# Encoder layer on one core: first operands of the down projection, the output projection's weights and a third table moved to earlier places

## The chip, the core and the metric

The kernel runs on one core of one Trainium2 chip. The metric is the device time in microseconds (us) of one execution; each kernel's time is the median of several. TensorE is written PE, VectorE DVE, ScalarE ACT, GpSimd POOL and SyncE SP, as in the rows. SP and POOL issue the transfers (DMA) between HBM and SBUF, each on a queue of its own.

## What is computed

A transformer-like encoder layer over 2560 tokens (512 of one request, 2048 of another) of width 1024, all in float32:

```python
def encoder_layer(x, w_in, w_fourier, sink_logits, w_out, ln_mix_g, ln_mix_b,
                  w_ff1, w_ff2, ln_ffn_g, ln_ffn_b):
    proj = x @ w_in
    ...
    heads = jnp.concatenate([fourier_mix(u, w_fourier),
                             windowed_attention(q, k, v, sink_logits)], axis=-1)
    x = layer_norm(DEEPNORM_ALPHA * x + heads @ w_out, ln_mix_g, ln_mix_b)
    h = jnp.square(jax.nn.relu(x @ w_ff1))
    x = layer_norm(DEEPNORM_ALPHA * x + h @ w_ff2, ln_ffn_g, ln_ffn_b)
    return x
```

`fourier_mix` is the real part of a 2-D DFT over positions and 128 channels, then a 128x128 map for each of four groups; `windowed_attention` has 8 query heads of 64 over 2 key and value heads, blocks of 128 tokens and a window of 128 to each side. The width of the hidden layer is 4096.

## The kernel before

It runs six stages one after the other, each with its own instruction streams, tiles and semaphores: `embed_project` (names a_), `fourier` (b_), `attend` (c_), `mix_out` (d_), `mlp_up` (u_) and `mlp_down` (e_). All orders are written out by hand, and semaphores alone say who waits. A stage ends when every engine has come to its end; SP comes to its end only when its last stores have landed. Then the stage's semaphores are cleared, all engines meet at a barrier, and the next stage begins. Few transfers cross such a border: those that a `load_...` function, handed over by `build`, issues into a tile that outlives a stage.

Each product of float32 matrices is made of three matmuls (`split_mm`, lines 63 to 65): both operands are split into a rounded part (hi, a cast on ACT) and a rest (lo, a subtraction on DVE). So an operand that lands in a raw tile needs one ACT and one DVE instruction before PE can use it.

**fourier.** Each of five units folds its 128 channels (`fold`: four DVE operations of half the length, two small ones, four more, `fold_low` splits the result), multiplies by a channel matrix on PE (`channels`, results z, four for each unit, each split by `z_high` and `z_low`), and then by tables of cosines and sines (`positions`). The first unit needs four table tiles of 128x2050, one after the other; each is loaded by POOL, rounded by `table_high` and split by `table_low`. The raw tables have two slots, so the third waits until `table_low` of the first is done.

**attend.** SP loads the bias (1.5 MB), then stores the results of 20 blocks. POOL loads the queries two blocks ahead.

**mix_out.** SP loads the output projection's eight weight tiles (0.5 MB each), POOL the heads' tile of 128 tokens and the tokens' x, two ahead. `product` takes 48 matmuls for 128 tokens, `norm` normalises, `transpose` and `mix_quarters` make the operands of the next stage. ACT and DVE first split the heads of block 0, then the eight weights, then the heads of block 1.

**mlp_up and mlp_down** are one level of Strassen's scheme (Winograd's form): seven products of sums of quarters. `mlp_up` goes through three groups of tokens, 16 pairs of hidden columns in each; `h_sums` on DVE makes four sums of each pair's results, and SP stores them. The sums of pair n are made and stored during pair n+1, those of the very last pair after it, ahead of the border. `mlp_down` is 336 steps, each with one 128x512 (or 384) piece of h and one 128x512 piece of weights in one of R = 8 raw slots; `load(n)` issues the two transfers, `high` and `low` split, and PE makes 12 matmuls of it (9 in later groups).

The border between these two, on the side of `mlp_up`'s SP:

```python
            store_sums(LAST, NP * len(UP_GROUPS) - 1, NP - 1)
            sp.wait_ge(h_sum_st, 16 * (NP * len(UP_GROUPS) + 1))
            for c in h_st:
                sp.wait_ge(h_st[c], 16 * (NP * len(UP_GROUPS) + 1))
```

## Time and profile before

| what | us |
|---|---|
| median of 3 runs (2564.68 to 2567.26) | 2567.06 |
| the profiled execution, its own time | 2564.25 |
| its span, first to last instruction | 2562.6 |
| PE busy in the span | 2402.4 |
| DVE busy | 1597.0 |
| ACT busy | 1094.0 |
| POOL busy | 179.4 |

The span is divided among the stages as follows, by the first instruction of each: fourier from 342 us, attend from 462.07 (SP's issue of the bias), mix_out from 690, mlp_up from 966, mlp_down from 1780. PE's matmuls are pipelined, so its busy time counts overlaps; what matters is where it stands idle and what ended the idle time, which is printed in brackets behind an instruction. "PEclk" is the granted clock of PE: 1.00 is 2.4 GHz and 0.50 is 1.2 GHz.

### The profile page before, as it was taken

What the parts mean: (1) busy time and instruction counts of PE and PEld (TensorE: products, weight loads), DVE (VectorE), ACT (ScalarE), POOL (GpSimd) and SP (SyncE); (2) the same over time, 40 slices, a digit from 0 to 9 for tenths busy, and PEclk for the clock granted to TensorE, in tenths of its full rate; (3) what the DMA queues carried; (4) which work ended last, traced back from release to release, by engine and by line L of the source; (5) the groups of instructions that cost most, each with busy time, mean ns of one, the idle gap of its engine ahead of it and who ended that gap; (6) DMA issues with size and microseconds to landing.
All of it is one profiled execution on the core that took longest, in us unless ns stands there. A gap on an engine that the chain in (4) does not pass through costs nothing. (4 is left out here: it accounts for less than half of the span.)

```text
span 2562.6 us, 35326 instructions
## 1 busy us (share of the span) xinstructions
PE 2402.4 (94%) x12192; PEld 2097.6 (82%) x12192; DVE 1597.0 (62%) x2220; ACT 1094.0 (43%) x1740; POOL 179.4 (7%) x246
## 2 busy tenths in 40 slices
PE   4999969899799987999999999997999999999998
PEld 3888859799678865888889999997888888888886
DVE  7544156666456567666676666665546577669667
ACT  2111123688611115444455555554433334544442
POOL 1000000222112210000000000000000011001001
PEclk9999979899899998999999999998999999999999
DMA  7665335322345665555577676665876659877974
GB/s 280 252 264 225 125 139 174 91 75 69 115 146 209 245 252 206 211 214 198 228 270 248 231 286 235 247 241 190 273 260 192 195 168 321 263 226 228 320 227 138
DMA packets 217624, 543.04 MB, mean 212 GB/s; under 512 B 21360, under 2 KB 89840, under 8 KB 198064
## 3 DMA queue, kind: packets, MB, share of 16 engines
q1 hardware_dynamic: 200208, 476.92, 53.4%
q0 software_dynamic: 17312, 64.76, 8.1%
q8 instruction: 61, 1.00, 0.2%
q14 instruction: 43, 0.35, 0.0%
HBM read 361.24 MB, written 180.36 MB: 211 GB/s over the span
## 5 line engine op out<-in xcount | busy, mean ns | idle before, releaser
L1794 DVE TENSOR_TENSOR e_lo<-e_raw,e_hi 128x896 fp32r<-128x896 f32 (+1 forms) x336 | 378.6, 1135 | 259.9 <-ACT e_hi L1777 251.8
L1777 ACT CAST e_hi<-e_raw 128x896 fp32r<-128x896 f32 (+1 forms) x336 | 330.4, 983 | 427.2 <-PE e_bank L65 380.5
L63 PE MATMUL e_bank<-e_hi,e_lo 128*128 128x512 f32 x1120 | 436.7, 390 | 15.6 <-DVE e_lo L1794 15.6
L65 PE MATMUL e_bank<-e_hi 128*128 128x512 f32 x1120 | 436.4, 390 | 0.0
L64 PE MATMUL e_bank<-e_lo,e_hi 128*128 128x512 f32 x1120 | 436.4, 390 | 0.0
L63 PE MATMUL u_bank<-u_x_hi,u_wa_lo 128*128 128x384 f32 (+1 forms) x768 | 274.2, 357 | 29.2 <-DVE u_x_first L1414 20.1
L65 PE MATMUL u_bank<-u_x_hi,u_wa_hi 128*128 128x384 f32 (+1 forms) x768 | 272.9, 355 | 0.0
L63 PEld LDWEIGHTS e_bank<-e_hi,e_lo 128*128 128x128 f32 x1120 | 210.7, 188 | 59.7 <-DVE e_lo L1794 15.9
L65 PEld LDWEIGHTS e_bank<-e_hi 128*128 128x128 f32 x1120 | 210.6, 188 | 43.9
L64 PEld LDWEIGHTS e_bank<-e_lo,e_hi 128*128 128x128 f32 x1120 | 210.7, 188 | 43.7
L63 PE MATMUL u_bank<-u_x_hi,u_wb_lo 128*128 128x384 f32 (+1 forms) x576 | 203.9, 354 | 8.3 <-DVE u_x_rest L1414 8.3
L64 PE MATMUL u_bank<-u_x_first,u_wa_hi 128*128 128x384 f32 (+1 forms) x576 | 205.1, 356 | 0.0
L65 PE MATMUL u_bank<-u_x_hi,u_wb_hi 128*128 128x384 f32 (+1 forms) x576 | 203.5, 353 | 0.0
L64 PE MATMUL u_bank<-u_x_rest,u_wb_hi 128*128 128x384 f32 (+1 forms) x576 | 203.5, 353 | 0.0
L63 PEld LDWEIGHTS u_bank<-u_x_hi,u_wa_lo 128*128 128x128 f32 x768 | 146.0, 190 | 41.7 <-issue 21.1
L65 PE MATMUL a_bank<-a_xt_hi,a_w_hi 128*128 128x512 f32 x400 | 159.6, 399 | 0.0
L64 PE MATMUL a_bank<-a_xt_lo,a_w_hi 128*128 128x512 f32 x400 | 157.6, 394 | 0.0
L63 PE MATMUL a_bank<-a_xt_hi,a_w_lo 128*128 128x512 f32 x400 | 157.3, 393 | 0.0
L65 PEld LDWEIGHTS u_bank<-u_x_hi,u_wa_hi 128*128 128x128 f32 x768 | 145.7, 190 | 10.3
L63 PE MATMUL d_mix<-d_w_hi,d_h_lo 128*128 128x512 f32 x320 | 128.4, 401 | 20.5 <-DVE d_w_lo L1224 20.5
L300 ACT ACTIVATE a_stage<-a_bank 128x512 f32<-128x512 f32 x50 | 29.9, 598 | 248.7 <-PE a_bank L65 248.7
L862 DVE CUSTOM_DVE_ANT_0 c_prob<-c_sc,c_bias,c_neg_sink 128x384 f32<-128x384 f32 (+1 forms) x160 | 93.9, 590 | 63.5 <-PE c_sc L962 43.5
(192 smaller groups left out, 4338.1 us busy)
## 6 DMA issues: line engine op xcount, KB each, us to landing
u_w_raw<-w_ff SPq DMA_DIRECT2D x48, 1024.0 KB, 7.8
e_raw<-s_t SPq DMA_DIRECT2D x192, 256.0 KB, 3.7
e_raw<-s_h SPq DMA_DIRECT2D x224, 192.0 KB, 2.8
e_raw<-w_ff SPq DMA_DIRECT2D x144, 256.0 KB, 3.9
u_w_sum<-s_ws SPq DMA_DIRECT2D x32, 1024.0 KB, 4.8
e_raw<-s_h SPq DMA_DIRECT2D x112, 256.0 KB, 2.8
s_h<-u_h_sum SPq DMA_DIRECT2D x32, 768.0 KB, 7.0
s_h<-u_h SPq DMA_DIRECT2D x96, 192.0 KB, 2.3
```

Source lines behind the costliest of these rows:

```text
L63: tensor.matmul(out, w_lo, m_hi, start=first, stop=False, skip_group_check=again)
L64: tensor.matmul(out, w_hi, m_lo, start=False, stop=False, skip_group_check=again)
L65: return tensor.matmul(out, w_hi, m_hi, start=False, stop=last, skip_group_check=again)
L300: act.mul(stage[:, m % 5, :], bank[:, m % 8, :], QSCALE if is_q else 1.0).then_inc(stage_done, 1)
L862: dve.tensor_tensor_reduce(prob[:, h % 4, 0:w], sc[:, h % 2, 0:w], bias[:, h, kbs[0] * P:kbs[0] * P + w], 1.0, neg_sink[:, h:h + 1], ALU.a ...
L1777: act.copy(part(hi, n), part(raw, n)).then_inc(hi_done, 1)
L1794: dve.tensor_tensor(part(lo, n), part(raw, n), part(hi, n).bitcast(F32), ALU.subtract).then_inc(split, 1)
```

## The change

- **fourier**: the raw tables get a third slot, in the tile of the values (`vt_raw`), which holds the channel matrices until `ab_split` 2. POOL loads the third table then, and the others when the table two before has been split. On ACT and DVE the order of the first unit's work is changed: `table_high(1)` stands ahead of the first `z_high`, and the first half of `fold(1)` stands between the third and the fourth `z_low`, ahead of `table_low(3)`.
- **attend and mix_out**: the eight weight tiles are loaded by `attend`'s SP, right behind the bias, into a tile `d_place` that both stages share. `mix_out` splits four weights, the heads of block 0, the other four weights, the heads of block 1. It uses the identity matrix that is already in SBUF, and its scratch lies in `d_place` and in the keys' tile.
- **mlp_up and mlp_down**: the two raw weight slots of `mlp_up` lie in the values' and the queries' tile, and become the raw slots 0 to 3 of `mlp_down`. In the last two pairs SP loads the first four steps of `mlp_down` into them. The last pair's sums are made by `mlp_down`'s DVE, behind `low(8)`, and stored by its SP, behind `load(20)`. The waits for the last stores of `mlp_up` stand in `mlp_down`, ahead of the first load of the last group.

The core of the difference (the rest passes tiles and semaphores along):

```diff
-                if n >= 2:
-                    pool.wait_ge(t_split, n - 1)
-                pool.dma_start(table(n)[2], table_ds[job][i * P:(i + 1) * P, :]).then_inc(t_ld[n % 2], 16)
+                if n == 2:
+                    pool.wait_ge(ab_split, 2)
+                elif n > 2:
+                    pool.wait_ge(t_split, n - 2)
+                pool.dma_start(table(n)[2], table_ds[job][i * P:(i + 1) * P, :]).then_inc(t_ld[n % 3], 16)
...
             fold(0)
             fold_low(0)
             table_low(0)
-            z_low(0, 0)
+            z_low_of(0, 0)
             table_low(1)
-            z_low(0, 1)
+            z_low_of(0, 1)
             table_low(2)
+            z_low_of(0, 2)
+            fold_once(1)
+            z_low_of(0, 3)
             table_low(3)
-            fold(1)
+            fold_twice(1)
             fold_low(1)
...
             table_high(0)
             copy_bias(0)
+            table_high(1)
             z_high(0, 0)
-            table_high(1)
+            table_high(2)
             z_high(0, 1)
-            table_high(2)
             table_high(3)
             fold_high(1)
...
             sp.dma_start(bias[:], bias_d).then_inc(bias_in, 16)
+            load_w_out(sp)
...
-            split_heads(0)
             for k in range(KT):
+                if k == KT // 2:
+                    split_heads(0)
                 act.wait_ge(w_ld[k], 16)
                 act.copy(w_hi[:, k, :], w_raw[k]).then_inc(w_hi_done, 1)
             split_heads(1)
...
-            rest_of_heads(0)
             for k in range(KT):
+                if k == KT // 2:
+                    rest_of_heads(0)
                 dve.wait_ge(w_hi_done, k + 1)
...
                     if not (g == LAST and isinstance(p, int) and p == NP - 2):
                         load_w(n + 2, s, 0 if isinstance(p, int) and p == NP - 2 else p + 2)
+                    else:
+
+                        sp.wait_ge(h_st[11], 16 * (NP + 1))
+                        load_down(sp, s)
                 elif g < LAST:
                     load_w(n + 2, s, 1)
+                else:
+                    load_down(sp, s)
...
-            store_sums(LAST, NP * len(UP_GROUPS) - 1, NP - 1)
-            sp.wait_ge(h_sum_st, 16 * (NP * len(UP_GROUPS) + 1))
-            for c in h_st:
-                sp.wait_ge(h_st[c], 16 * (NP * len(UP_GROUPS) + 1))
...
-            h_sums(NP * len(UP_GROUPS) - 1, UP_GROUPS[LAST][1])
...
+def load_step(sp, step, slot, loaded, h_d, w2_d, t_d):
+
+    raw = {"B11": 0, "B21": 2, "B22": 3}
+    g, j, k = step
+    size, col = UP_GROUPS[g][1], first_pair(g) * P
+    _, a, b = DOWN_ORDER[j]
+    sp.dma_start(slot[:, 512 - size:512], h_d[H_ORDER.index(a), k * P:(k + 1) * P, col:col + size]).then_inc(loaded, 16)
+    src, at = (w2_d, raw[b]) if b in raw else (t_d, T_ORDER.index(b))
+    sp.dma_start(slot[:, 512:1024], src[k * P:(k + 1) * P, at * 512:at * 512 + 512]).then_inc(loaded, 16)
...
+            def store_last_sums():
+                size, col = UP_GROUPS[LAST][1], first_pair(LAST) * P
+                sp.wait_ge(h_summed, 1)
+                sp.dma_start(h_d[3:7, FF // 2 - P:FF // 2, col:col + size].rearrange("s p c -> p s c"),
+                             h_sum[:, :, 0:size]).then_inc(h_sum_st, 16)
...
-                load(n)
+                if (g, j, k) == (LAST, 0, 0):
+                    sp.wait_ge(h_sum_st, 16 * (NK * len(UP_GROUPS) + 1))
+                    for c in h_st:
+                        sp.wait_ge(h_st[c], 16 * (NK * len(UP_GROUPS) + 1))
+                if n >= len(raw_first):
+                    load(n)
+                if n == 20:
+                    store_last_sums()
...
+            def last_sums():
+
+                w = UP_GROUPS[LAST][1]
+                dve.wait_ge(h_sum_st, 16 * NK * len(UP_GROUPS))
+                dve.tensor_tensor(h_sum[:, 0, 0:w], h[:, 0, 1, 0:w], h[:, 1, 1, 0:w], ALU.add)
+                dve.tensor_tensor(h_sum[:, 2, 0:w], h[:, 0, 0, 0:w], h[:, 0, 1, 0:w], ALU.subtract)
+                dve.drain()
+                dve.tensor_tensor(h_sum[:, 1, 0:w], h_sum[:, 0, 0:w], h[:, 0, 0, 0:w], ALU.subtract)
+                dve.drain()
+                dve.tensor_tensor(h_sum[:, 3, 0:w], h[:, 1, 0, 0:w], h_sum[:, 1, 0:w], ALU.subtract
+                                  ).then_inc(h_summed, 1)
...
                 if n == R:
+                    last_sums()
                     dve.wait_ge(const_in, 32)
...
+                def load_w_out(sp):
+                    for k in range(KT):
+                        sp.dma_start(place[:, k * D:(k + 1) * D], d["w_out"][k * P:(k + 1) * P, :]
+                                     ).then_inc(w_out_ld[k], 16)
...
+            raw_first = [tile.rearrange("p b c -> p (b c)")[:, half * D:(half + 1) * D] for tile in w_raw for half in range(2)]
+
+            def load_down(sp, slot):
+                for n in (2 * slot, 2 * slot + 1):
+                    load_step(sp, (0, 0, n), raw_first[n], op_ld[n], s["h"], d["w_ff2"], s["t"])
```

DVE in fourier, from the second table's split (`b_t_lo` is a table's rest, `b_z_lo` a z's, `c_q_raw` and `b_ends` are written by the first half of a fold, `b_u_raw` by the second). Before:

```order
L490 TENSOR_TENSOR b_t_lo<-c_k_raw,b_t_hi 128x2050
L496 TENSOR_TENSOR b_z_lo<-b_bank,b_z_hi 128x512 x2
L490 TENSOR_TENSOR b_t_lo<-c_k_raw,b_t_hi 128x2050 x2
L458 TENSOR_TENSOR c_q_raw<-b_u_raw 128x512
L459 TENSOR_TENSOR c_q_raw<-b_u_raw 128x512
L461 TENSOR_TENSOR c_q_raw<-b_u_raw 128x512
L462 TENSOR_TENSOR c_q_raw<-b_u_raw 128x512
L463 TENSOR_TENSOR b_ends<-b_u_raw 128x1
L464 TENSOR_TENSOR b_ends<-b_u_raw 128x1
L467 TENSOR_TENSOR b_u_raw<-c_q_raw 128x512
```

and in the changed kernel:

```order
L500 TENSOR_TENSOR b_t_lo<-c_vt_raw,b_t_hi 128x2050
L509 TENSOR_TENSOR b_z_lo<-b_bank,b_z_hi 128x512
L465 TENSOR_TENSOR c_q_raw<-b_u_raw 128x512
L466 TENSOR_TENSOR c_q_raw<-b_u_raw 128x512
L468 TENSOR_TENSOR c_q_raw<-b_u_raw 128x512
L469 TENSOR_TENSOR c_q_raw<-b_u_raw 128x512
L470 TENSOR_TENSOR b_ends<-b_u_raw 128x1
L471 TENSOR_TENSOR b_ends<-b_u_raw 128x1
L509 TENSOR_TENSOR b_z_lo<-b_bank,b_z_hi 128x512
L500 TENSOR_TENSOR b_t_lo<-c_k_raw,b_t_hi 128x2050
L477 TENSOR_TENSOR b_u_raw<-c_q_raw 128x512
```

The z of the first unit are now split between the tables, and the first half of the second unit's fold stands ahead of the fourth table's split instead of behind it.

ACT at the start of mix_out (`d_h_hi` are the heads' rounded parts, `d_w_hi` the weights'). Before:

```order
L1147 CAST d_h_hi<-d_h_raw 128x1024
L1166 CAST d_w_hi<-d_mixed 128x1024 x7
L1166 CAST d_w_hi<-d_w_last 128x1024
L1147 CAST d_h_hi<-d_h_raw 128x1024 x3
L1155 COPY d_mixed<-d_turn 128x512
```

and now:

```order
L1178 CAST d_w_hi<-d_place 128x1024 x4
L1158 CAST d_h_hi<-d_h_raw 128x1024
L1178 CAST d_w_hi<-d_place 128x1024 x4
L1158 CAST d_h_hi<-d_h_raw 128x1024 x3
L1166 COPY d_place<-d_turn 128x512
```

Four of the weights stand ahead of the heads of block 0; on DVE the rests stand in the same order.

SP around the end of mlp_up (`s_h` is the hidden layer in HBM; in the changed kernel `c_k_raw` holds the results and sums, `c_vt_raw` and `c_q_raw` the raw slots). Before:

```order
L1349 DMA u_w_sum<-s_ws 128x2048
L1364 DMA s_h<-u_h_sum 128x4x384
L1358 DMA s_h<-u_h 128x384 x3
L1364 DMA s_h<-u_h_sum 128x4x384
L1358 DMA s_h<-u_h 128x384 x3
L1364 DMA s_h<-u_h_sum 128x4x384
L1280 UNCONDITIONAL_BRANCH
L1706 UNCONDITIONAL_BRANCH
L1715 DMA e_raw<-s_h 128x512
L1721 DMA e_raw<-w_ff 128x512
L1715 DMA e_raw<-s_h 128x512
L1721 DMA e_raw<-w_ff 128x512
```

and now:

```order
L1355 DMA u_w_sum<-s_ws 128x2048
L1662 DMA c_vt_raw<-s_h 128x512
L1664 DMA c_vt_raw<-w_ff 128x512
L1662 DMA c_vt_raw<-s_h 128x512
L1664 DMA c_vt_raw<-w_ff 128x512
L1370 DMA s_h<-c_k_raw 128x4x384
L1364 DMA s_h<-c_k_raw 128x384 x3
L1662 DMA c_q_raw<-s_h 128x512
L1664 DMA c_q_raw<-w_ff 128x512
L1662 DMA c_q_raw<-s_h 128x512
L1664 DMA c_q_raw<-w_ff 128x512
L1370 DMA s_h<-c_k_raw 128x4x384
```

Eight transfers of mlp_down stand ahead of the stores of the last two pairs, four in each, and the store of the last sums no longer stands ahead of the stage's end.

## Rows read from the trace of the kernel before

**Rows 1.** The page, busy time of PE, share of the span, instructions:

```profile
PE 2402.4 (94%) x12192; PEld 2097.6 (82%) x12192; DVE 1597.0 (62%) x2220; ACT 1094.0 (43%) x1740; POOL 179.4 (7%) x246
```

**Rows 2.** Timeline of PE: start, duration, instruction, [idle before <-releaser]:

```profile
374.29 0.39 PE L63 MATMUL b_bank<-b_t_hi,b_z_lo 128*128 128x258 f32 x1 [2.87 <-DVE b_t_lo L490]
380.86 0.37 PE L63 MATMUL b_bank<-b_ends_hi,b_ab_lo 128*128 128x2 f32 x1 [4.06 <-DVE b_f_lo L484]
...
702.88 0.77 PE L63 MATMUL d_mix<-d_w_hi,d_h_lo 128*128 128x512 f32 x1 [16.86 <-DVE d_w_lo L1224]
...
1787.21 0.80 PE L63 MATMUL e_bank<-e_hi,e_lo 128*128 128x512 f32 x1 [15.57 <-DVE e_lo L1794]
```

**Rows 3.** Timeline of DVE, first unit of fourier:

```profile
362.28 2.29 DVE L490 TENSOR_TENSOR b_t_lo<-c_k_raw,b_t_hi 128x2050 fp32r<-128x2050 f32 x1 [1.10 <-ACT b_t_hi L573]
...
374.16 0.69 DVE L458 TENSOR_TENSOR c_q_raw<-b_u_raw 128x512 f32<-128x512 f32 x1
...
376.86 0.69 DVE L467 TENSOR_TENSOR b_u_raw<-c_q_raw 128x512 f32<-128x512 f32 x1
...
379.59 2.35 DVE L484 TENSOR_TENSOR b_f_lo<-b_u_raw,b_f_hi 128x1024 fp32r<-128x1024 f32 x2
```

**Rows 4.** Timeline of ACT, first unit of fourier:

```profile
360.34 1.90 ACT L573 CAST b_t_hi<-c_k_raw 128x2050 fp32r<-128x2050 f32 x1
...
364.98 0.58 ACT L579 CAST b_z_hi<-b_bank 128x512 fp32r<-128x512 f32 x1 [1.97 <-PE b_bank L65]
...
370.01 1.90 ACT L573 CAST b_t_hi<-c_k_raw 128x2050 fp32r<-128x2050 f32 x1 [2.64 <-DMA c_k_raw<-table]
```

**Rows 5.** Timeline of ACT, start of mix_out:

```profile
699.30 1.04 ACT L1147 CAST d_h_hi<-d_h_raw 128x1024 fp32r<-128x1024 f32 x1 [12.65 <-DMA d_h_raw<-s_heads]
700.25 5.04 ACT L1166 CAST d_w_hi<-d_mixed 128x1024 fp32r<-128x1024 f32 x5
```

**Rows 6.** Timeline of DVE, start of mix_out:

```profile
701.52 5.76 DVE L1224 TENSOR_TENSOR d_w_lo<-d_mixed,d_w_hi 128x1024 fp32r<-128x1024 f32 x5
...
723.11 1.29 DVE L1189 SCALAR_TENSOR_TENSOR d_y<-d_xn,d_mix 128x512 f32<-128x512 f32 x2 [7.93 <-PE d_mix L65]
...
734.00 1.28 DVE L1189 SCALAR_TENSOR_TENSOR d_y<-d_xn,d_mix 128x512 f32<-128x512 f32 x2 [3.65 <-PE d_mix L65]
```

**Rows 7.** The heads' transfers: issue on POOL, landing of that one, of 720:950:

```profile
690.40 0.90 POOL L1109 DMA_DIRECT2D d_h_raw<-s_heads  x1 [29.66 <-POOLq L80]
...
d_h_raw<-s_heads POOLq DMA_DIRECT2D x1, 512.0 KB, 8.9
...
DMA to landing us min/median/max: 5.5/7.6/14.5
```

**Rows 8.** Stretches of 2 us: PE busy, PEclk, DMA share, GB/s:

```profile
376.00:378.00 2.00, 0.80 (x2) 0.50 0.00 0
...
704.00:706.00 2.00, 2.00 (x7) 0.52 1.02 404
...
1790.00:1792.00 2.00, 2.00 (x8) 0.66 1.05 390
```

**Rows 9.** Border of mlp_up and mlp_down: ACT, SP (issue, landing), DVE:

```profile
1772.82 0.52 ACT L1550 ACTIVATE u_h<-u_h 128x384 f32<-128x384 f32 x1
...
1775.82 0.38 SPq L1364 DMA_DIRECT2D s_h<-u_h_sum  x1
1780.39 0.35 SPq L1715 DMA_DIRECT2D e_raw<-s_h  x1
...
s_h<-u_h_sum SPq DMA_DIRECT2D x1, 768.0 KB, 3.5
...
1785.93 1.22 DVE L1794 TENSOR_TENSOR e_lo<-e_raw,e_hi 128x1024 fp32r<-128x1024 f32 x1 [10.21 <-ACT e_hi L1777]
```

**Rows 10.** Start of attend: DVE, and the bias from issue to landing:

```profile
463.17 6.61 DVE L849 TENSOR_TENSOR c_kb<-c_k_raw,c_ka 128x1024 fp32r<-128x1024 f32 x5 [0.87 <-ACT c_ka L913]
...
c_bias<-bias SPq DMA_DIRECT2D x1, 1536.0 KB, 6.3
```

More of the change, by code:

```diff
@@ L345, in fourier @@
         ab_lo = al.sb("ab_lo", [P, 2, FOUR], F32R)
-        t_raw = k_raw[:].rearrange("p v t -> p (v t)")[:, 0:2 * WIDE].rearrange("p (s w) -> p s w", s=2)
+        t_raw = [*(k_raw[:].rearrange("p v t -> p (v t)")[:, s * WIDE:(s + 1) * WIDE] for s in range(2)), vt_raw]
         t0_hi = al.sb("t0_hi", [P, 1, FOUR + 2], F32R)
@@ L695, in _, with attend @@
                     channels(n + 1, 1)
-def attend(nc, bias_d, ident, operands, load_queries, heads_d):
+def attend(nc, bias_d, ident, operands, load_queries, heads_d, load_w_out):
     AHEAD = {"scores": 6, "bias": 5, "exp": 4, "turn": 3, "high": 2, "rest": 1, "values": 0}
@@ L1071, in mix_out @@
         heads_v = heads_d.rearrange("(k p) t -> p k t", p=P)
-        w_raw = [*(mixed.rearrange("p s j c -> p (s j c)")[:, k * D:(k + 1) * D] for k in range(KT - 1)), w_last[:]]
+        w_raw = [place[:, k * D:(k + 1) * D] for k in range(KT)]
         block = ctx.enter_context(nc.Block())
@@ L1083, in _ @@
         def _(sp):
-            for k in range(KT):
-                sp.dma_start(w_raw[k], w_out[k * P:(k + 1) * P, :]).then_inc(w_ld[k], 16)
-            sp.dma_start(gain[:], ln_g.partition_broadcast(P)).then_inc(const_in, 16)
-            sp.dma_start(shift[:], ln_b.partition_broadcast(P)).then_inc(const_in, 16)
-            sp.dma_start(ident[:], ident_d).then_inc(const_in, 16)
+            sp.dma_start(gain, ln_g.partition_broadcast(P)).then_inc(const_in, 16)
+            sp.dma_start(shift, ln_b.partition_broadcast(P)).then_inc(const_in, 16)
             for n in range(NT):
@@ L1269, in _, with mlp_up @@
             transpose(NT - 1)
-def mlp_up(nc, xb_d, w1_d, ws_d, h_d, first):
+def mlp_up(nc, xb_d, w1_d, ws_d, h_d, first, h_st, h_sum_st, load_down):
     NP = FF // (2 * P)
@@ L1671, in mlp_down @@
         mhalf = al.sb("mhalf", [P, 1])
-        raw = al.sb("raw", [P, R, 1024])
+        raw_rest = al.sb("raw", [P, R - len(raw_first), 1024])
+        raw = [*raw_first, *(raw_rest[:, s, :] for s in range(R - len(raw_first)))]
         hi = al.sb("hi", [P, R, 1024], F32R)
@@ L1698, in part @@
         def part(tile, n):
-            return tile[:, n % R, 512 - UP_GROUPS[steps[n][0]][1]:1024]
+            return (raw[n % R] if tile is raw else tile[:, n % R, :])[:, 512 - UP_GROUPS[steps[n][0]][1]:1024]
         def token_rows(g, half, t):
@@ L1940, in build @@
-        q_raw = ctx.enter_context(nc.sbuf_tensor("c_q_raw", [P, 2, NH, P], F32))
-        q_ld = [nc.alloc_semaphore(f"c_q_ld{slot}") for slot in range(2)]
-        q_view = s["proj"][FOUR:KROW, :].rearrange("(h d) t -> d h t", d=HD)
-        def load_queries(pool, b, slot=None):
-            slot = b if slot is None else slot
-            for half in range(2):
-                pool.dma_start(q_raw[half * HD:(half + 1) * HD, slot, :, :], q_view[:, :, bass.ds(b * P, P)]
-                               ).then_inc(q_ld[slot], 16)
@@ L1949, in build @@
-        fourier(nc, s["proj"], (chan, wf, in_ld), k_raw, q_raw, [d["table0"], d["table1"]], s["heads"],
-                load_keys_values, load_queries)
-        attend(nc, d["bias"], ident, (k_raw, vt_raw, q_raw, snk, k_ld, v_ld, q_ld, snk_in), load_queries, s["heads"])
-    with ExitStack() as ctx:
-        x_first = ctx.enter_context(nc.sbuf_tensor("u_x_first", [P, 3, 4 * 512], F32))
-        w_first = ctx.enter_context(nc.sbuf_tensor("u_w_raw", [P, 2, 4, 512], F32))
-        x_ld = [nc.alloc_semaphore(f"u_x_first_ld{j}") for j in range(3)]
-        w_ld = [nc.alloc_semaphore(f"u_w_ld{slot}") for slot in range(2)]
-        def load_w_first(sp):
-            for p in range(2):
-                sp.dma_start(w_first[:, p, :, :], d["w_ff1"][p * P:(p + 1) * P, :].rearrange("p (b c) -> p b c", b=4)
-                             ).then_inc(w_ld[p], 16)
-        def load_x_first(pool):
-            for j in range(3):
-                pool.dma_start(x_first[:, j, :].rearrange("p (q c) -> p q c", q=4),
-                             s["xb"][0:4, :, j, :].rearrange("q p c -> p q c")).then_inc(x_ld[j], 16)
-        mix_out(nc, s["x_norm"], s["heads"], d["w_out"], d["ln_mix_g"], d["ln_mix_b"], d["ident"], s["x1"], s["xb"],
-                load_x_first, load_w_first)
-        mlp_up(nc, s["xb"], d["w_ff1"], s["ws"], s["h"], (x_first, w_first, x_ld, w_ld))
```

150 lines of the change are left out of this document (89 added, 61 removed).

## The prediction, made before the changed kernel was run

> **What bounds the kernel now.** I read the page first: PE is busy for 94% of the span, the next engine, DVE, for 62% [rows 1]. So PE's work sets the time, and the change takes no matmul away; it can only shorten what PE stands idle or runs slowly. The next view was PE's timeline, for its longest idle times, which stand near the borders of stages. The change touches four of them: 2.87 and 4.06 us in the first unit of fourier, 16.86 us ahead of mix_out and 15.57 us ahead of mlp_down [rows 2]. Last I read the other engines around each, to see which chain ends last there. The reader should see that each of the four ends with a DVE rest (`b_t_lo`, `b_f_lo`, `d_w_lo`, `e_lo`), and that behind the last two stands a transfer that was issued only after the border. Between these places PE waits for almost nothing, so what is won at one of them is kept to the end, if the next chain moves along with it.
>
> **Fourier.** The fourth table's rest ends at 374.16, where the fold of the second unit begins [rows 3]; its rounding began at 370.01, after 2.64 us of waiting for the transfer [rows 4]. With a third slot the third table is loaded before the first z is there, and the fourth as soon as the first is split. ACT has rounded the second z at 360.34, begins the third table there as it did the second [rows 4], and ends at 362.24. DVE splits this table from 362.28, where it now splits the second [rows 3]; that takes 2.2 to 2.3 us, so to 364.5. The third z's rest costs 0.6, the first half of the fold 374.16 to 376.86 less a drain, 2.6 [rows 3], the fourth z's rest 0.6: 368.3. The fourth z is rounded at 365.5, and the fourth table by 367.4 (1.90) [rows 4], ahead of DVE. Its rest takes DVE from 368.3 to 370.5. Then comes the second half of the fold, and from 376.86 to PE's start at 380.86 it is 4.0 us [rows 2, 3]: PE starts the second unit's channels at 374.6. That is **6.2 us** earlier. The unit's end is also what PE waits for next, and all that follows there is PE's own work or stands behind it, so I keep all 6.2. Bounds: 4 if the second unit's own load, which now shares its bandwidth with the third table, comes 2 us after DVE wants it; 11 if PE's clock stays up (a rival below).
>
> **Start of mix_out.** Now PE waits until 702.88 for the first weight's rest [rows 2]. The heads of block 0 are rounded at 699.30, when they have landed, and five weights behind them from 700.25 [rows 5]; the rest come with their transfers, and the first block's product ends only at 723.11 [rows 6]. Changed: the weights have landed long before. ACT rounds four from 690 to 694 (about 1.0 each, 5.04 for five) [rows 5], DVE splits them at 1.15 each (5.76 for five) [rows 6], and both then wait for the heads. These were issued at 690.40 and took 8.9 us beside 4 MB of weights; later ones take 5.5 to 14.5, median 7.6, nearly each behind another transfer in POOL's queue [rows 7]. The first is alone in its queue, with 1 MB of gain and shift on the other, so I take 6.2, nearest to the fast ones: landed at 696.6, rounded 697.7, rest 698.9, PE starts at 699.1. The other four weights pass ACT and DVE at 1.0 and 1.15 us each, and PE takes 0.68 (3 matmuls of 0.227, from 10.9 us for the 48 of block 1, 723.11 to 734.00 [rows 6]), or 1.36 at the low clock, so it doesn't outrun them. The clock: PE started at 702.88 and was at the low level until about 705.9; at 1787.21 the same lasted to about 1791.4 [rows 2, 8]. Four us at half speed lose 2. The product of block 0 takes 10.9 + 2.0 = 12.9 and ends at 712.0, **11.0 us** before 723.1 (3.8 from the start, the rest from the weights that came one by one). Bounds: 8.4 with the heads at 8.9 again, 11.8 with 5.5. The identity matrix is needed only after block 2's product, and the normalisation of block 0 waits for gain and shift until after 712, so both stay hidden.
>
> The Trainium skill ("DMA: Bandwidth & Descriptors", section "Anatomy of one DMA — SWDGE (gpsimd) path") fits a transfer of POOL's with about 2.0 us plus the bytes at 436 GB/s, so an estimate of 3.2 us for these 512 KB. No transfer of heads in this trace is that fast; by the page the sum of this stage would be the one of the rival "heads at once".
>
> **What the weights' transfers cost in attend.** SP issues them behind the bias, eight issues, ahead of nothing but the first block's store, which comes 30 us later. The bias is issued with the stage's first instruction, at 462.07, and lands after 6.3, at 468.4; DVE is busy with the keys until 469.78 [rows 10] and asks for it then. It stands first in its queue, so I charge nothing; if it lands 1.4 us later the cover is gone, and each further us is one of PE's. I take 3 us as the far end, half its own duration. POOL's query loads meet the 4 MB for some 10 us, but they are issued a block ahead of their use. A rule against the change is the same page's, section "Queues, rings and completion order": an engine takes turns between the queues it has work for. By it the first two query loads might take twice as long, which a block of 10 us would still hide; only the heads' 8.9 us beside the weights [rows 7] points the same way.
>
> **Border of mlp_up and mlp_down.** Now: ACT's last square ends at 1773.34, DVE's sums follow, the store is issued at 1775.82 and lands 3.5 later, at 1779.3; the barrier costs 1.1, and SP issues the first operands at 1780.39 [rows 9]. Their rest begins at 1785.93, PE at 1787.21 [rows 2, 9]. Changed: ACT's square is the last thing that the stage waits for, since SP has no wait left. With 1.1 to 1.6 for the barrier (I take 1.4) ACT begins at 1774.8 with operands that landed in the last pairs. One cast 1.0, one rest 1.22, and PE starts at 1777.3: **9.9 us** earlier. Bounds: 10.3 and 8.5, if SP's last stores held it for another 1.4. The four steps in hand are 10.9 us of PE's work at full clock, and the fifth step's load, issued at 1775, needs about the 4.5 us of the first one now (from 1780.39 to one cast of 1.0 ahead of 1785.93). So there is no second wait. The eight extra issues of about 0.4 us each (0.35 and 0.38 [rows 9]), four in each of the last two pairs, stand ahead of the stores of sums, which wait for DVE anyway. The last sums cost DVE four operations of 0.56 and two drains at the ninth step, with seven steps in hand; if that cover were missing it would be 2.5 us. The waits moved to the last group are long fulfilled there.
>
> **The sum.** 6.2 + 11.0 + 9.9 = 27.1. The profiled execution took 2564.25 (span 2562.6), 2.8 below the median of 2567.06. 2564.25 - 27.1 = 2537.15, and with the 2.8 it is **2540.0** for a median. Its own range is 2536 to 2544: the bounds of the three terms, less likely all on one side.
>
> **Rivals.**
> - *The clock stays up in fourier.* Then PE's idle time ahead of the second unit's channels, some 2.6 us instead of 4.06, would not drop it. In the trace the gap of 2.87 already did: from 376 PE is at 0.50 [rows 8], which speaks against. Worth half of what would run low: two z of 2.56 each (1.97 and 0.59 between the casts [rows 4]) and four us of dense work behind them, as at the other starts. That is 4.6 more, 2535.
> - *The heads and the bias are late.* The heads land after 8.9 as now (11.0 becomes 8.4), and the bias costs one or two: 2544. For it: only one transfer of heads on a quiet queue would prove my 6.2, and the trace has none.
> - *Heads at once.* If they land before the four weights are split, DVE ends the heads' rest at about 696.5, and PE starts 2.6 earlier: 2537.4. Nothing in the trace is that fast.
> - *Fourier's gain is given back*, the change not doing there what it says: DVE stands at the first half of the fold for the second unit's load, and all behind it on DVE waits, the fourth table too. From 6 us late on, nothing is left: 2546.
> - *Slower.* The results and sums of mlp_up move into the keys' tile, and its raw weights into two others. If their engines met there, each of the 48 pairs would be longer. It decides at 27.1 / 48 = 0.56 us a pair; at 0.7 it is 2573.6. Nothing in the trace shows that a tile's place costs anything, and DVE has a third of its time free.
>
> **How the numbers follow.** Forecast 0.60, clock 0.12, late 0.14, heads at once 0.04, given back 0.07, slower 0.03. The range takes in all but the slower case and the far tails: 2533 to 2548. A measurement here tells 0.2%, about 5 us, from no change; all cases but the last are far beyond it. Faster 0.96, same 0.01, slower 0.03.
>
> **What would show it.** PE's idle time ahead of mix_out near 13 us, not 16.86, and no wait inside the first product; ahead of mlp_down near 6 us, ended by a rest that no transfer precedes; in fourier the fold's second half next to the fourth table's rest and one gap of about 2.6; the bias still landing before DVE asks. Wrong would be: a new idle time at the first block of attend, heads landing after 8 us, or ACT starting mlp_down well after 1775 on the old clock, because something else holds the barrier.

## The result, and the profile after

The changed kernel took 2541.72 us (median of 4 runs, 2536.99 to 2542.62), the kernel before 2567.16 (2564.68 to 2567.88) beside it: ratio 0.9899, 95% interval 0.9882 to 0.9916, so 25.4 us faster. The profiled execution took 2542.19, its span 2540.5, which is 22.1 shorter than the 2562.6 of the kernel before. The forecast was 2540.0. The 3.3 us between 25.4 and 22.1 are a matter of their own, below.

PE's timeline of the changed kernel answers to [rows 2]: start, duration, instruction, [idle before <-releaser]:

```profile
374.48 0.37 PE L63 MATMUL b_bank<-b_ends_hi,b_ab_lo 128*128 128x2 f32 x1 [2.36 <-DVE b_f_lo L494]
...
692.87 0.79 PE L63 MATMUL d_mix<-d_w_hi,d_h_lo 128*128 128x512 f32 x1 [13.69 <-DVE d_h_lo L1192]
...
954.50 0.77 PE L63 MATMUL u_bank<-u_x_hi,u_wa_lo 128*128 128x512 f32 x1 [17.75 <-DVE u_x_first L1422]
...
1291.83 0.41 PE L63 MATMUL u_bank<-u_x_hi,u_wb_lo 128*128 128x384 f32 x1 [2.70 <-DVE u_x_rest L1422]
...
1764.22 0.79 PE L63 MATMUL e_bank<-e_hi,e_lo 128*128 128x512 f32 x1 [4.94 <-DVE e_lo L1829]
```

One of fourier's two gaps is gone and the other is 2.36 instead of 4.06; mix_out waits 13.69 instead of 16.86, now for the heads' rest and no longer for a weight's; the border costs 4.94 instead of 15.57. The idle time ahead of mlp_up, which the change leaves alone, is 17.75, and before it was 17.98, at 971.18: it moved along as a whole. Where PE's first matmul of each part starts, in this and in second traces of both kernels (experiments, below), gives the table by stage. A column is one trace:

| us | before | before, second | after | after, second |
|---|---|---|---|---|
| start of attend | 462.12 | 461.01 | 455.28 | 455.44 |
| attend, with the gap behind it | 240.76 | 240.83 | 237.59 | 237.81 |
| mix_out, with the gap behind it | 268.30 | 267.57 | 261.63 | 261.26 |
| mlp_up, first group | 323.46 | 324.60 | 324.57 | 324.46 |
| second group | 244.26 | 245.77 | 245.88 | 245.73 |
| third group and border | 248.31 | 250.18 | 239.27 | 239.27 |
| mlp_down to the span's end | 775.39 | 775.94 | 776.28 | 776.23 |

The first row holds what stands ahead of fourier too: PE's first matmul of fourier starts at 342.01, 342.31, 341.87 and 343.81 in the four traces, and up to there nothing was changed. From that matmul to attend it is 120.11, 118.70, 113.41 and 111.63.

Against the first trace of before, the lead at attend is 6.84, mix_out adds 3.17 + 6.67 = 9.84, and the border is in the 9.04 of the last group. But the first two groups of mlp_up, whose work the change left alone but for where tiles lie, are 1.11 and 1.62 longer, and of the 10.63 won at the border's gap the last group shows 1.59 less. That was not in the forecast, and the later experiments go after it.

VectorE in the first unit of fourier, changed kernel, answers to [rows 3]:

```profile
364.95 0.68 DVE L465 TENSOR_TENSOR c_q_raw<-b_u_raw 128x512 f32<-128x512 f32 x1
...
368.10 2.28 DVE L500 TENSOR_TENSOR b_t_lo<-c_k_raw,b_t_hi 128x2050 fp32r<-128x2050 f32 x1
370.47 0.69 DVE L477 TENSOR_TENSOR b_u_raw<-c_q_raw 128x512 f32<-128x512 f32 x1
...
373.20 2.36 DVE L494 TENSOR_TENSOR b_f_lo<-b_u_raw,b_f_hi 128x1024 fp32r<-128x1024 f32 x2
```

The reader is to see an engine without a gap: from 364.35 on, the rows in between included, each begins where the one before ends. The fourth table's rest no longer waits for a table that has yet to land, and the second half of the fold stands right behind it. DVE's own work is now what PE's 2.36 us wait for.

Start of mix_out: the heads' issue on POOL, ACT's and DVE's timelines, answering to [rows 5 to 7]:

```profile
683.50 0.90 POOL L1120 DMA_DIRECT2D d_h_raw<-s_heads  x1 [29.61 <-POOLq L80]
...
683.07 3.88 ACT L1178 CAST d_w_hi<-d_place 128x1024 fp32r<-128x1024 f32 x4 [3.28 <-PEq L80]
690.51 1.04 ACT L1158 CAST d_h_hi<-d_h_raw 128x1024 fp32r<-128x1024 f32 x1 [3.55 <-DMA d_h_raw<-s_heads]
691.46 3.88 ACT L1178 CAST d_w_hi<-d_place 128x1024 fp32r<-128x1024 f32 x4
...
692.73 4.62 DVE L1237 TENSOR_TENSOR d_w_lo<-d_place,d_w_hi 128x1024 fp32r<-128x1024 f32 x4
...
706.76 1.28 DVE L1201 SCALAR_TENSOR_TENSOR d_y<-d_xn,d_mix 128x512 f32<-128x512 f32 x2 [8.28 <-PE d_mix L65]
```

The heads come 7.0 us after their issue, ACT has stood for 3.55 by then, and behind them nothing waits for a transfer. The border, ACT and DVE, answers to [rows 9]:

```profile
1760.46 0.52 ACT L1557 ACTIVATE c_k_raw<-c_k_raw 128x384 f32<-128x384 f32 x1
1761.86 1.99 ACT L1800 CAST e_hi<-c_vt_raw 128x1024 fp32r<-128x1024 f32 x2 [0.88 <-PEq L80]
...
1762.94 2.36 DVE L1829 TENSOR_TENSOR e_lo<-c_vt_raw,e_hi 128x1024 fp32r<-128x1024 f32 x2 [3.07 <-ACT e_hi L1800]
```

Between the last square's end (1760.98) and the first cast stand 0.88 us. Stretches of 2 us behind the two starts (PE busy, granted clock, DMA share, GB/s), answering to [rows 8]:

```profile
696.00:698.00 2.00, 2.00 (x6) 0.50 0.47 158
698.00:700.00 2.00, 2.00 (x9) 0.84 0.00 0
...
1768.00:1770.00 2.00, 2.00 (x6) 0.50 1.04 393
1770.00:1772.00 2.00, 2.00 (x10) 0.90 1.07 392
```

PE ran at 1.2 GHz for about 5.8 us from 692.87 and 6.2 us from 1764.22. In the first trace of before it was 3.1 and 4.2 us, in the second 4.6 and 5.4; in the second trace of after 5.0 and 6.0.

### The profile page after: what moved, and what is told of

The parts are those of the page before. It is cut to its first block and busy times, and to the rows that moved or that the text cites. A ratio compares the mean times of both kernels' runs of the same rounds, so it can differ in the third digit from the quotient of the medians.

```text
span 2540.5 us, 35321 instructions
## 1 busy us (share of the span) xinstructions
PE 2401.3 (95%) x12192; PEld 2099.1 (83%) x12192; DVE 1595.9 (63%) x2220; ACT 1092.7 (43%) x1740; POOL 180.3 (7%) x246
## 5 line engine op out<-in xcount | busy, mean ns | idle before, releaser
L1829 DVE TENSOR_TENSOR e_lo<-e_raw,e_hi 128x896 fp32r<-128x896 f32 (+1 forms) x168 | 189.3, 1134 | 123.3 <-ACT e_hi L1800 122.2
L1800 ACT CAST e_hi<-e_raw 128x896 fp32r<-128x896 f32 (+1 forms) x168 | 165.2, 983 | 212.1 <-PE e_bank L65 201.5
L65 PEld LDWEIGHTS u_bank<-u_x_hi,u_wa_hi 128*128 128x128 f32 x768 | 145.9, 190 | 10.2
L1829 DVE TENSOR_TENSOR e_lo<-c_q_raw,e_hi 128x896 fp32r<-128x896 f32 (+1 forms) x84 | 94.8, 1134 | 66.5 <-ACT e_hi L1800 66.5
```

Source lines behind the costliest of these rows:

```text
L65: return tensor.matmul(out, w_hi, m_hi, start=False, stop=last, skip_group_check=again)
L1800: act.copy(part(hi, n), part(raw, n)).then_inc(hi_done, 1)
L1829: dve.tensor_tensor(part(lo, n), part(raw, n), part(hi, n).bitcast(F32), ALU.subtract).then_inc(split, 1)
```

## The experiments

Theory: four places, each won by taking a transfer from the path, add up. The rivals: the moved splits do it, not the loads; one of the two holds at the border would be enough; fourier's gain is given back later. Medians are of 4 to 15 runs. The kernel before stood at 2567.65 us beside after_again, fourier_old, wout_late and down_late, at 2566.5 beside heads_first, sums_in_up, warm_turn and warm_starts, and at 2568.34 beside the last two. So only the first group has a median of the changed kernel beside it.

**after_again**, the changed kernel once more, for a second trace and a median on the chip of fourier_old, wout_late and down_late.

> The changed kernel once more, as the base for the others on the same chip. Theory (the gain is the sum of four PE idle times that got shorter, less what PE's granted clock loses behind other pauses): median 2540 to 2543, single runs between 2537 and 2543, because the drop of the clock behind a pause of 2 to 4 us comes in some executions and not in others. Rival (the 4 us that mlp_up lost are a steady cost of the moved tiles): no run below 2540.

Measured: 2538.78 us (2537.54 to 2541.83), ratio 0.9888 (0.9873 to 0.9903). That agrees with the first measurement within the intervals; it also shows that two medians of one kernel differ by 3 us, so a single term of 2 us can't be read from them, but from the traces. The median is 1.2 below the expected 2540 to 2543, and three of the four runs are below 2540, so the rival of a steady cost falls. The expectations of fourier_old, wout_late and down_late had been worked out from about 2541.7; all three measured times lie below them, by 1.3 to 4.0.

**fourier_old**, one part undone: the whole function `fourier` as before (two slots for tables, the fold whole and behind the fourth table).

> Fourier as before (two raw slots for the tables, old order on ACT and DVE), all else changed. Theory (the stages' gains add up): the next stage begins 6.8 us later, 2548 to 2549. Rival (the fourier part is hidden or given back later): within 1.5 us of the changed kernel, 2541 to 2543.

Measured: 2546.69 us (2545.07 to 2548.32), ratio 0.9921 (0.9908 to 0.9935), 7.9 slower than after_again. In its trace PE has both gaps of [rows 2] back:

```profile
374.54 0.39 PE L63 MATMUL b_bank<-b_t_hi,b_z_lo 128*128 128x258 f32 x1 [2.87 <-DVE b_t_lo L490]
...
381.11 0.37 PE L63 MATMUL b_bank<-b_ends_hi,b_ab_lo 128*128 128x2 f32 x1 [4.29 <-DVE b_f_lo L484]
```

The second unit's channels start 6.6 us later than in the changed kernel, attend at 460.93, and attend and mix_out together, the later groups of mlp_up and mlp_down take what they take in after_again within 0.2 us (the first group is 0.8 shorter). From PE's first matmul of fourier to attend it is 118.68 us, 7.1 more than in after_again. The gain of fourier is not given back.

**wout_late**, one part undone: the eight weight tiles are loaded by mix_out's SP again; the new order of the splits is kept.

```diff
             sp.dma_start(bias[:], bias_d).then_inc(bias_in, 16)
-            load_w_out(sp)
...
         def _(sp):
+            load_w_out(sp)
             sp.dma_start(gain, ln_g.partition_broadcast(P)).then_inc(const_in, 16)
```

> The output projection's weights are loaded at the start of mix_out again, the new order of the splits stays. Theory (the weights' transfers delay both the heads and each weight): heads land after about 9 us instead of 7.0, PE starts 2 us later and then waits for the weights, 9 to 10 us in all, 2551. Rival (the new order of the splits is what gained): 2542 to 2544.

Measured: 2547.02 us (2543.99 to 2547.29), ratio 0.9917 (0.9903 to 0.993), 8.2 slower than after_again. ACT's timeline shows what it waits for:

```profile
687.10 1.04 ACT L1178 CAST d_w_hi<-d_place 128x1024 fp32r<-128x1024 f32 x1 [6.92 <-DMA d_place<-w_out]
...
693.96 1.04 ACT L1178 CAST d_w_hi<-d_place 128x1024 fp32r<-128x1024 f32 x1 [1.56 <-DMA d_place<-w_out]
694.91 1.04 ACT L1158 CAST d_h_hi<-d_h_raw 128x1024 fp32r<-128x1024 f32 x1
697.48 1.04 ACT L1178 CAST d_w_hi<-d_place 128x1024 fp32r<-128x1024 f32 x1 [1.53 <-DMA d_place<-w_out]
```

The weights come one by one, the heads are there without a wait, and PE idles 17.89 us ahead of mix_out, more than before the change: with late weights the new order makes PE start later. But from attend's start to mlp_up's it takes 506.22 us, which is 7.1 more than in the changed kernel (499.22 and 499.07) and still 2.2 to 2.8 less than before (509.06 and 508.40). So the loads carry about 7 of mix_out's term, and 2.2 to 2.8 come with the rest of the edit (order of the splits, no load of the identity matrix, other places for the scratch); these aren't separated. The expected 2551 was too much by 4.0, of which 2.9 are the base of after_again.

**heads_first**, the other part undone: weights loaded beside attention, heads of block 0 split ahead of them.

```diff
+            split_heads(0)
             for k in range(KT):
-                if k == KT // 2:
-                    split_heads(0)
                 act.wait_ge(w_ld[k], 16)
```

(and `rest_of_heads(0)` likewise on DVE).

> The changed kernel with one part undone: in the out projection the first heads are split ahead of the weights' pieces again, as in the kernel before, while the weights are still loaded beside attention. Theory A, that the gain ahead of the out projection comes from the weights' early load and the moved split only uses it: ScalarE and VectorE now wait for the heads' landing (690.5 in the changed kernel's trace) with no weight split, TensorE's first product needs the first weight's low part, which stands behind the heads' low part (1.23 us) and its own (1.16 us, a quarter of 4.62), and each later step of the product brings 1.16 us of VectorE against 12.9 / 8 = 1.6 us of TensorE: TensorE starts some 1.2 us later, and the time is 2541 us (2540 to 2543) beside 2538.8 to 2540 for the changed kernel. Theory B, that the split's new place carries half of the term: 4.6 us or more later, 2544.5 us.

Measured: 2540.82 us (2538.21 to 2541.87), ratio 0.9901 (0.9886 to 0.9916).

```profile
689.73 1.04 ACT L1158 CAST d_h_hi<-d_h_raw 128x1024 fp32r<-128x1024 f32 x1 [10.79 <-DMA d_h_raw<-s_heads]
...
693.31 0.77 PE L63 MATMUL d_mix<-d_w_hi,d_h_lo 128*128 128x512 f32 x1 [15.00 <-DVE d_w_lo L1235]
```

PE starts mix_out on a weight's rest, 3.6 us after the heads' landing; in both traces of the changed kernel it is 2.4. The idle time alone would prove less: sums_in_up and warm_turn, which leave mix_out alone, show 15.23 and 15.25, because their heads took 8.5 us to land instead of 7.0. Theory A holds: with early weights, the split's order is worth the 1.2 that one DVE rest takes, and the medians can't show even that.

**down_late**, one part undone: the first four steps' operands loaded behind the border, last sums still made in mlp_down.

```diff
-                        sp.wait_ge(h_st[11], 16 * (NP + 1))
-                        load_down(sp, s)
...
-                if n >= len(raw_first):
-                    load(n)
+                load(n)
```

> The first four steps' operands are loaded behind the border again, the last sums stay in mlp_down. Theory: of the 10.6 us won there, the time from issue to landing (4.5 us at the first step) is due to the early loads, the other 6 to the sums and their store that no longer hold the border: 2546, PE's idle time ahead of mlp_down 9 to 10 us. Rival (the early loads are nearly all of it): 2550 or more.

Measured: 2544.55 us (2542.13 to 2547.14), ratio 0.9912 (0.9899 to 0.9926), 5.8 slower than after_again. SP issues at 1759.72 and ACT's first cast waits for the landing:

```profile
1759.72 0.34 SPq L1656 DMA_DIRECT2D c_vt_raw<-s_h  x1
...
1764.18 1.04 ACT L1793 CAST e_hi<-c_vt_raw 128x1024 fp32r<-128x1024 f32 x1 [5.30 <-DMA c_vt_raw<-w_ff]
...
1766.53 0.80 PE L63 MATMUL e_bank<-e_hi,e_lo 128*128 128x512 f32 x1 [9.37 <-DVE e_lo L1822]
```

PE's gap is 9.37 instead of 4.94: 4.4 for the loads.

**sums_in_up**, the converse: operands loaded in mlp_up, last sums made, stored and waited for ahead of the border (on SP the lines quoted in the section on the kernel before; on DVE the last `h_sums`; `mlp_down` makes and stores none).

> The changed kernel with one part undone: the last group's sums of h are made and stored in the up projection again and the stage's end waits for their store, while the first operands of the down projection's first four steps are still loaded in the up projection. Theory A, that the border's gain is the sum of two parts (down_late gave 5.8 of the 10.6 us back): the store and the sums bring the remaining 4.8 us back, 2544.5 us (2543 to 2546). Theory B, that either part alone holds the border (the two holds ran side by side before): this alone gives back nearly as much as both together, 8 us or more, 2548 us.

Measured: 2546.74 us (2544.48 to 2548.2), ratio 0.9922 (0.9908 to 0.9935).

```profile
693.62 1.04 ACT L1158 CAST d_h_hi<-d_h_raw 128x1024 fp32r<-128x1024 f32 x1 [5.08 <-DMA d_h_raw<-s_heads]
...
1763.32 0.38 SPq L1370 DMA_DIRECT2D s_h<-c_k_raw  x1
...
1767.89 1.99 ACT L1803 CAST e_hi<-c_vt_raw 128x1024 fp32r<-128x1024 f32 x2 [7.04 <-PEq L80]
...
1770.25 0.80 PE L63 MATMUL e_bank<-e_hi,e_lo 128*128 128x512 f32 x1 [11.10 <-DVE e_lo L1832]
```

From the store's issue to ACT's cast it is 4.6 us. The gap is 11.10, so sums and store are worth 6.2; with the 4.4 of down_late that makes 10.6, and before and after differ by 15.57 - 4.94 = 10.6. The two holds stood one behind the other; theory B, that either holds the border alone, is refuted by the gap, which would be 13 us or more by it. The median doesn't decide: it lies between the two expectations, 8.0 above that of after_again, with no changed kernel beside it. The expected 4.8 had been worked out with the median's 5.8 for the loads, where the trace has 4.4. In the profiled execution some 1.5 us more are the late heads of mix_out; why the median stands as high as it does was not followed up.

**warm_turn**, for the loss in mlp_up. Matmuls that the layer doesn't need, in a gap of each group's first pair:

```diff
+                    if start and j == 4:
+                        pe.wait_ge(c_done[21], n + 1)
+                        for _ in range(20 if g == 0 else 12):
+                            pe.matmul(bank[:, s, BANK["P4"], 0:w].rearrange("p (q c) -> p q c", c=P),
+                                      wa_hi[:, s, 0, 0:P], x_hi[:, 0, 0:w // P, 0, :], start=True, stop=True)
```

> The changed kernel with added matmuls that aren't the reference's (their bank is overwritten by the product behind them): 20 in the first group of the up projection and 12 in each of the others, in the idle gap of TensorE ahead of the fifth product of a group's first pair (2.70 us at 1291.83, 2.00 us at 1536.96 in the changed kernel's trace). Theory A, that the 1.2 to 1.6 us that each group of the up projection lost against the kernel before is the granted clock, at 1.2 GHz for some 4 us behind this gap in the changed kernel and at 2.4 GHz there in the kernel before: the clock stays up, the stages of the up projection between TensorE's starts get 1.2 to 1.6 us shorter each, in all up to 4.3 us, 2535.5 us (2534.5 to 2537.5). Theory B, that the moved tiles or the DMA queues cost this time: no stage gets shorter, 2539.5 to 2541 us.

Measured: 2539.04 us (2535.91 to 2540.43), ratio 0.989 (0.9875 to 0.9905). The first two groups take 322.90 and 243.90 us, 1.7 and 2.0 less than in the changed kernel, and less than before the change too; the third takes 240.00, 0.7 more. The median misses the expected 2534.5 to 2537.5, and the time of the whole is not told from the changed kernel's. The mechanism is there, its worth in the median is not.

**warm_starts**: nine matmuls of 128x512 in float32 ahead of mix_out's first product, three of 128x384 at mlp_down's start, which the layer doesn't need either.

```diff
+            pe.wait_ge(w_ld[0], 16)
+            for _ in range(9):
+                pe.matmul(mix[:, 0, 0, :], w_raw[0][:, 0:P], w_raw[0][:, 0:512], start=True, stop=True)
             product(0)
...
+            for _ in range(3):
+                pe.matmul(bank[:, 0, 0, 0:384], h[:, 0, 0, 0:P], h[:, 0, 0, 0:384], start=True, stop=True)
```

> The changed kernel with added matmuls that aren't the reference's (what they write is overwritten): 9 ahead of the out projection's first product, 3 at the down projection's start. Theory A, that what is left of the gain at these two places is the clock behind the idle time (TensorE at 1.2 GHz for 5.8 us from 692.87 and 6.0 us from 1764.22): the clock is up when the first product starts, which saves up to 2.9 us ahead of the out projection where TensorE is the bound and less where its product waits for VectorE's splits, and up to 3 us in the down projection: 2536.5 us (2534.5 to 2538.5). Theory B, that at both places VectorE's splits set the pace however fast TensorE is: 2539 to 2541 us.

Measured: 2536.62 us (2536.35 to 2536.75), ratio 0.9883 (0.9868 to 0.9898). The granted clock from the first useful matmul on:

```profile
693.00:695.00 2.00, 1.87 (x8) 1.00 0.41 156
1762.00:1764.00 2.00, 2.00 (x10) 1.00 0.64 178
```

mix_out takes 259.64 us from PE's first useful matmul, 1.6 to 2.0 less than in the two traces of the changed kernel. The same stage varies by itself, though: without the idle time behind it, it is 241.89 here and 241.76 in warm_both, against 242.88 to 243.89 in six traces with the changed mix_out and no added matmuls there. So it is 1.0 to 2.1 us, and DVE's splits alone don't set the pace there. mlp_down takes 773.37 us from its first useful matmul, 2.9 less than the 776.28 and 776.23 of the changed kernel. The median is the lowest of all, but the interval overlaps with that of after_again: the medians don't show the gain.

**warm_both**, both edits together.

> The changed kernel with the added matmuls of both earlier kernels: ahead of the out projection's first product, at the down projection's start, and in the first pair of each group of the up projection. If the granted clock is what both bought, the gains add: warm_starts stands at 2536.6 us, and its up projection (324.65 and 246.16 us between the first starts of the groups) has room to the 322.90 and 243.90 us of warm_turn: 1.75 + 2.26 = 4 us, some of it lost to the third group, 2533.5 us (2532 to 2536). If TensorE's idle time is only filled and something else sets the pace, nothing is added: 2536.6 us.

Measured: 2536.92 us (2535.17 to 2537.86), ratio 0.9877 (0.9862 to 0.9893). The expected 2533.5 did not come, and the median is that of warm_starts. The trace shows what became of it: mlp_up's groups took 323.15, 243.81 and 239.74 us, as in warm_turn and 2.2 less in sum than in warm_starts. But the heads took 8.8 us to land and PE's first useful matmul of mix_out stood 1.30 idle us, the idle time ahead of mlp_up was 19.20 instead of 17.75, and at the border the clock fell during the added matmuls, for 3.4 us. From attend's start to mlp_up's it is 500.39 us, 2.3 more than in warm_starts. Whether the three other runs have the same isn't known.

**before_again**, the kernel before, for a second trace.

> The kernel before, unchanged, for a second trace of it. Theory A, that the up projection's 1.2 to 1.6 us a group are lost to a second low stretch of the clock, which comes in some executions of either kernel: the stages between TensorE's starts may differ here from 323.46 and 244.26 us by such steps (up to 324.6 and 246), with the low stretch at the second gap of the first pair there or not. Theory B, that the kernel before never has it and the change brought it: 323.5 and 244.3 us again, within 0.1.

Measured: 2567.53 us (2565.93 to 2570.47), ratio 1.0 (0.9991 to 1.0009); span 2565.9. Its first two groups take 324.60 and 245.77 us, as in the changed kernel. The turn to the second group, once in each trace of the kernel before. The first trace (stretches of 2 us):

```profile
1298.00:1300.00 2.00, 2.00 (x8) 0.54 0.91 381
...
1306.00:1308.00 2.00, 0.59 (x3) 1.00 1.02 372
1308.00:1310.00 2.00, 2.00 (x13) 1.00 0.10 35
```

and the second:

```profile
1297.00:1299.00 2.00, 2.00 (x13) 0.99 0.65 262
...
1305.00:1307.00 2.00, 0.22 (x1) 1.00 1.03 377
1307.00:1309.00 2.00, 2.00 (x8) 0.57 0.29 104
```

PE's gap in the middle of that pair, by the timelines of the first and of the second trace:

```profile
1307.41 0.41 PE L63 MATMUL u_bank<-u_x_hi,u_wb_lo 128*128 128x384 f32 x1 [1.77 <-DVE u_x_rest L1414]
```

```profile
1306.78 0.41 PE L63 MATMUL u_bank<-u_x_hi,u_wb_lo 128*128 128x384 f32 x1 [2.76 <-DVE u_x_rest L1414]
```

In both, PE starts the group after 3.91 idle us (at 1294.64 and 1294.01), and starts again behind DVE's rest 12.77 us later. In the first, PE is at 1.2 GHz for some five us from its start, arrives late at the gap, stands 1.77, and the clock stays at 2.4 GHz. In the second the clock is back some three us after the start, PE arrives early, stands 2.76, and the clock falls again for three us of dense work. So the kernel of before has the loss as well; theory A holds. heads_first, with the mlp_up of the changed kernel, shows the short form again (323.51 and 244.36). But it is the only one of eight traces with that mlp_up whose second group is short; the other seven take 245.7 to 246.2, and before it is one of two. Whether the change makes the long form more frequent is not shown.

## Why the prediction came out right

**What it stood on.** "Between these places PE waits for almost nothing" is not so: ahead of mlp_up stands an idle time of 17.98 us, longer than any of the four. It did no harm, since it was 17.75 afterwards, but it had to move along for the sum to hold, and the prediction didn't ask whether it would.

**Fourier, 6.2.** PE started the second unit's channels at 374.48 where 374.6 was worked out, and every DVE row stands within 0.3 us of the sum. The lead at attend was 6.84, and 5.6 between the second traces, but there fourier itself began 1.50 later in after, in a part that nothing changed. From PE's first matmul of fourier the gain is 6.7 in the first pair of traces and 7.1 in the second: 6.2 was 0.5 to 0.9 too low. Behind the gap PE was at 1.2 GHz until 384.6 (384.2 in the second trace), so the rival "the clock stays up" fell, as [rows 8] had spoken for. The rival had priced some 9 us at the low level there; they were 10.2 and 6.8. "Given back" fell by fourier_old.

**Start of mix_out, 11.0.** It was 9.84 (9.33 between the second traces), inside its bounds. The mechanism held: four weights split ahead of the heads, a wait for one transfer, none inside the product. Two of its numbers were too good. The heads took 7.0 us on a queue with nothing ahead, not the 6.2 taken "nearest to the fast ones", which costs 0.8. And "four us at half speed" were 5.8, another 0.9 at half. That would leave 9.3; the other 0.5 was not followed up. "Heads at once" fell with the 7.0. In part this was luck: of nine traces with the weights loaded early, six have the first heads landing after 6.9 to 7.3 us and three after 8.5 to 8.8 (sums_in_up, warm_turn, warm_both), and what ran ahead of them in these three is the changed kernel's code, but for warm_both's added matmuls. "Heads landing after 8 us" was a sign of being wrong, and those three show it: there the term is some 1.5 smaller, and the heads' half of "the heads and the bias are late" is true of them. The estimate of 3.2 us by the Trainium skill ("DMA: Bandwidth & Descriptors", section "Anatomy of one DMA — SWDGE (gpsimd) path") is less than half of it; the measurement decides. The loads of x, of the same size on the same queue, took a median of 3.9 us in this trace. A row of the heads' transfer is 512 bytes, one of x's 4096; that this makes the difference was not tested.

**Attend, 0.** With mix_out's gap taken off, attend lasts 240.76 - 16.86 = 223.90 before and 237.59 - 13.69 = 223.90 after. The bias landed 6.5 us after its issue instead of 6.3, still 1.2 ahead of the cover's end. The eight weight loads took a median of 10.0 us each and nobody waited. The first two query loads met them. Number, size and median landing of these two, before and after:

```profile
c_q_raw<-s_proj POOLq DMA_DIRECT2D x2, 256.0 KB, 4.5
...
c_q_raw<-s_proj POOLq DMA_DIRECT2D x2, 256.0 KB, 8.6
```

That is the "twice as long" that the prediction had reckoned with, and the block hid it as it said.

**Border, 9.9.** PE's gap shrank by 10.6. The step that was off is the barrier, taken at 1.4: the trace has 0.88. mlp_down took 0.9 longer than in the first trace of before: the clock stayed low for 6.2 us from the start, where it had been 4.2 there. Most of that isn't the change's, since in the second trace of before it stayed low for 5.4, and between the second traces mlp_down took only 0.3 longer.

**mlp_up, 0.** Right as a cost of the change: in the short form the first two groups, 16 pairs each, take 323.51 and 244.36 us with the moved tiles (heads_first) against 323.46 and 244.26, so the "slower" rival (0.56 us a pair) had no trace at all. Wrong as a reading of one execution: the trace of before on which the sum stood was one without a second fall of the clock, and the profiled execution of after had it in the second group and in the third. In the first group it was another stretch: behind the gap of 3.9 us in the first pair (979.93, before 996.61) PE ran 5.4 us at 1.2 GHz instead of 2.8. That is 1.62 + 1.59 + 1.11 = 4.3 us, enough for the 3.3 by which the difference of the spans (22.1) fell short of that of the medians (25.4). The second traces, which both have it, differ by 2565.9 - 2540.2 = 25.7, where 27.1 was forecast; there the terms measured 7.1 for fourier less 1.5 for its late begin, 9.3, 10.9 with the third group, 0.2 for the first two groups and -0.3 for mlp_down.

So by this pair mix_out stood 1.7 too high, fourier 0.9 and the border 1.0 too low. The three terms make 27.3 where 27.1 was forecast: the sum came out as well as it did because the errors are of both signs. What can't be settled here: why the clock's return after the same 3.9 us of idle time takes three us in one execution and five in another.

## What to carry to other kernels

A border costs what its holds cost one behind the other: here a sum, its store and the wait for its landing (6.2 us), and the first load after it (4.4). Each can be taken away alone: load the next stage's first operands into tiles that are free a pair earlier, and let the next stage make the last results where it has steps in hand. When the big transfers are gone from a stage's start, what is left is the one that can't be issued earlier; put the engines' other work ahead of it, which is worth the length of what would else stand behind it (one DVE rest here, 1.2 us).

Before a difference of one or two us in one trace is put down to a change, take a second trace of the kernel before, since a stage can have two lengths in one kernel. Measure each stage from its own first matmul, so that what varied ahead of it stays out, and a wait from the landing that ends it.

## What was not expected of the hardware

- The same idle time of PE, 3.91 us at 1294, was followed by five us at 1.2 GHz in one execution and three in the next, of one and the same kernel; with a second gap behind it the shorter return cost more in the end (245.77 against 244.26 us for the group). The traces of the changed mlp_up agree: a second gap of 2.6 to 2.8 us with a fall of the clock behind it in seven, 1.66 without one in heads_first.
- One and the same 512 KB transfer of heads, first in its queue with the same transfers issued behind it, took 6.9 to 7.3 us in six traces and 8.5 to 8.8 in three. Beside the 4 MB of weights it took 8.9, 8.3 and 8.3. What sets it is open.
- The length of the low clock behind a start isn't set by the idle time ahead of it alone. After the same 4.94 us at the border the changed kernel had 6.2 and 6.0 us at 1.2 GHz, and heads_first about 4.7 from 1760.95. The stretch of heads_first (PE busy, granted clock, DMA share, GB/s), at 1.00 from 5 us behind its start, where the changed kernel, from 1768 to 1770, still had 0.50:

```profile
1764.00:1766.00 2.00, 2.00 (x7) 0.59 1.00 366
1766.00:1768.00 2.00, 2.00 (x10) 1.00 1.08 398
```

- With 128x512 matmuls in float32 ahead of mix_out's start the clock was at 2.4 GHz from the first useful matmul on (1.00 from 693 to 695), and the stage got 1.0 to 2.1 us shorter, in two traces. With three of 128x384 ahead of the border's it was up in warm_starts (1.00 from 1762 to 1764) and had fallen to 1.2 GHz in warm_both.
